# Latent attention in a hybrid decoder layer: values projected in token order, keys in a bank of their own, a new order of splits, and all ten turns of a head's probabilities behind the gate

## What is computed

```python
q = (rms_norm(c_q, q_norm) @ w_uq).reshape(b, s, MLA_HEADS, QK_NOPE + QK_ROPE)      # 8 heads, 64 + 32
q_nope, q_pe = q[..., :QK_NOPE], q[..., QK_NOPE:]
q_pe = apply_rope(q_pe, cos[:, :, None], sin[:, :, None])
kv = (rms_norm(c_kv, kv_norm) @ w_ukv).reshape(b, s, MLA_HEADS, QK_NOPE + V_DIM)    # 64 + 64
k_nope, v = kv[..., :QK_NOPE], kv[..., QK_NOPE:]
...
y_a = causal_dense_attention(q_full, k_full, v, (QK_NOPE + QK_ROPE) ** -0.5) @ w_br_mla
```

## Time and profile before

| | |
|---|---|
| median of 3 runs | 1281.73 us (1281.72 to 1281.84) |
| the profiled execution | 1280.79 us, its span 1279.0 us |
| PE busy | 1267.3 us (99%) |
| DVE, ACT, POOL busy | 669.7, 441.7, 18.8 us |

### The profile page before, as it was taken

One profiled execution on the slowest core, in us unless ns is written; L12 is line 12 of the kernel. 1 busy time (PEld: TensorE's weight loads), 2 busy tenths in 40 slices (PEclk: granted clock), 3 DMA queues, 4 the chain that ended last, 5 costly groups with the idle time before them and its releaser, 6 DMA issues.

```text
span 1279.0 us, 16611 instructions
## 1 busy us (share of the span) xinstructions
PE 1267.3 (99%) x5998; PEld 1033.5 (81%) x5998; DVE 669.7 (52%) x984; ACT 441.7 (35%) x763; POOL 18.8 (1%) x36
## 2 busy tenths in 40 slices
PE   9999999999999999999999999999999999999997
PEld 6888888888888777788888888888888888888886
DVE  6744444433336677475665746675644444443323
ACT  6233332322233444343343424423433332232221
POOL 0000000000000000300000000000000000000000
PEclk9999999999999999999999999999999999999999
DMA  6342223333322221622222231222322322233321
GB/s 214 101 111 98 98 98 98 90 91 95 103 92 71 64 70 66 132 67 83 79 78 92 66 99 51 97 89 95 99 96 98 98 98 98 98 90 92 93 88 66
DMA packets 36003, 118.38 MB, mean 93 GB/s; under 512 B 4680, under 2 KB 4680, under 8 KB 35968
## 3 DMA queue, kind: packets, MB, share of 16 engines
q1 hardware_dynamic: 34416, 114.83, 27.8%
q0 software_dynamic: 1264, 3.06, 1.5%
q10 hardware_dynamic: 288, 0.03, 0.0%
HBM read 115.36 MB, written 2.55 MB: 92 GB/s over the span
## 4 chain that ended last, share of the span: by engine, by line
PE 94%; DVE 2%; DMA 1%; issue 1%; ACT 1%; SPq 0%; DVEq 0%; ACTq 0%
PE bank L542 36%; PE bank L376 17%; PE bank L378 17%; PE bank L377 17%; PE bank L725 1%; PE bank L751 1%; PE bank L645 1%; PE bank L672 1%; DVE mla_stats L1451 1%; DMA x<-in_x_t 1%; PE bank L661 1%; PE bank L769 1%; PE bank L765 1%; DMA const<-in_tables 0%; ACT w_hi L358 0%
## 5 line engine op out<-in xcount | busy, mean ns | idle before, releaser
L363 DVE TENSOR_TENSOR w_lo<-raw,w_hi 128x1024 fp32r<-128x1024 f32 (+2 forms) x221 | 258.8, 1171 | 227.6 <-ACT w_hi L358 225.4
L358 ACT ACTIVATE w_hi<-raw 128x1024 fp32r<-128x1024 f32 (+2 forms) x221 | 224.3, 1015 | 433.3 <-PE bank L542 228.3
L542 PE MATMUL bank<-act_hi,w_hi 128*128 128x512 f32 x704 | 218.5, 392 | 0.3 <-DVE w_lo L363 0.3
L542 PE MATMUL bank<-act_hi,w_lo 128*128 128x512 f32 x704 | 217.0, 389 | 0.0
L542 PE MATMUL bank<-act_lo,w_hi 128*128 128x512 f32 x704 | 216.9, 389 | 0.0
L376 PE MATMUL bank<-act_hi,w_hi 128*128 128x512 f32 x528 | 210.7, 399 | 2.0 <-DVE w_lo L363 1.2
L378 PE MATMUL bank<-act_hi,w_lo 128*128 128x512 f32 x528 | 206.2, 390 | 0.0
L377 PE MATMUL bank<-act_lo,w_hi 128*128 128x512 f32 x528 | 205.9, 390 | 0.0
L542 PEld LDWEIGHTS bank<-act_hi,w_hi 128*128 128x128 f32 x704 | 132.2, 188 | 29.6 <-DVE w_lo L363 1.0
L542 PEld LDWEIGHTS bank<-act_hi,w_lo 128*128 128x128 f32 x704 | 132.2, 188 | 27.5
L542 PEld LDWEIGHTS bank<-act_lo,w_hi 128*128 128x128 f32 x704 | 132.2, 188 | 27.4
(11 more groups left out here) (177 smaller groups left out, 1049.3 us busy)
## 6 DMA issues: line engine op xcount, KB each, us to landing
raw<-in_ffn_up SPq DMA_DIRECT2D x87, 512.0 KB, 3.3
raw<-in_w_dil SPq DMA_DIRECT2D x40, 512.0 KB, 3.3
raw<-in_ffn_down SPq DMA_DIRECT2D x32, 448.0 KB, 3.3
raw<-in_ffn_down SPq DMA_DIRECT2D x16, 512.0 KB, 3.5
raw<-in_w_mla_gates SPq DMA_DIRECT2D x8, 512.0 KB, 3.3
raw<-in_w_branches SPq DMA_DIRECT2D x8, 512.0 KB, 3.3
raw<-in_w_out SPq DMA_DIRECT2D x8, 512.0 KB, 3.2
raw<-in_w_latent SPq DMA_DIRECT2D x6, 512.0 KB, 3.3
```

The source lines that it names most:

```text
L358: nc.scalar.activation(w_hi[:, s % SPLIT, 0:tiles * P], raw[:, s % RAW, 0:tiles * P], ACT.Copy).then_inc(hi_ready, 1)
L363: nc.vector.tensor_tensor(w_lo[:, s % SPLIT, 0:tiles * P], raw[:, s % RAW, 0:tiles * P], w_hi[:, s % SPLIT, 0:tiles * P].bitcast(F32), ALU ...
L542: last = nc.tensor.matmul(out, w[:, s % SPLIT, tile * P:(tile + 1) * P], moving[:, row, :], start=row == 0 and w is w_hi and moving is act_hi,
```

## The change

All values are now projected at once before head 0, with the latents as the stationary operand, so that they come out in token order (`values`, 24 products into banks 5, 6, 2, 3) and are scaled and copied by ACT (`take_values`). The transposes of values and the tensor `mla_vt` are gone. The first of two heads projects keys for both (6 products into bank 7, which `attend` uses as well); queries always go to bank 0 and gates to bank 1. The ten transposes of a head's probabilities all stand behind the gate, in banks 5, 6 and 0. ACT splits the next gate's piece before the tanh; in even heads DVE takes the query before it normalizes; in the last head the split of the second dilated piece moves ahead of exponentials and normalizing. In the first SwiGLU the split of piece 4 moves ahead by half a turn. The loop over heads is written out.

```diff
+            def values():
+                s = PIECES["mla"]
+                pe.wait_ge(lo_ready, s + 1)
+                pe.wait_ge(chunk_taken, CHUNKS["latent"] + 4)
+                for b, out in enumerate((5, 6, 2, 3)):
+                    block_of = slice(b * P, (b + 1) * P)
+                    for k in range(KKV):
+                        hi, lo = (w[:, s % SPLIT, k * SEQ:(k + 1) * SEQ] for w in (w_hi, w_lo))
+                        latent, rest = (part[:, KQ + k, block_of] for part in (lat_hi, lat_lo))
+                        nc.tensor.matmul(bank[out][:, :], latent, hi, start=k == 0, stop=False)
+                        nc.tensor.matmul(bank[out][:, :], latent, lo, start=False, stop=False)
+                        last = nc.tensor.matmul(bank[out][:, :], rest, hi, start=False, stop=k == KKV - 1)
...
+            def lora(h):
+                s = lora_piece(h)
+                pe.wait_ge(lo_ready, s + 1)
+                if h % 2 == 0:
+                    if h == 0:
+                        pe.wait_ge(mean_ready, 2)
+                    elif h > 2:
+                        pe.wait_ge(mixed_taken, h // 2 - 1)
+                    multiply(s, range(KQ, LORA_TILES), bank[7][:, :], ...).then_inc(inner_done, 1)
+                c = query_chunk(h)
+                free_chunk(pe, c)
+                if h > 1:
+                    pe.wait_ge(turned_taken, 3 * (h - 1))
+                multiply(s, range(KQ), bank[c % 2][:, :], ...).then_inc(piece_done, 1)
-            def turn_values(h, i):
...
             def turn_probs(h, part):
+                unit = 3 * h + part
+                pe.wait_ge(mla_scaled, 4 * h + 4)
+                if h:
+                    pe.wait_ge(turned_taken, unit - 2)
+                if part == 2:
+                    pe.wait_ge(chunk_taken, (query_chunk(h + 1) if h < MLA_HEADS - 1 else CHUNKS["dil"]) + 1)
...
             def attend(h):
+                if h < MLA_HEADS - 1:
+                    pe.wait_ge(keys_taken, h // 2 + 2)
                 for key in range(BLOCKS):
...
-                    pe.wait_ge(turned_taken, 4 * h + 2 + part + 8 * i)
+                    pe.wait_ge(turned_taken, 3 * h + 1 + part)
...
             def attention(h):
                 score(h)
-                turn_values(h, i)
-                def turn_early(k):
-                    if k == 6:
-                        turn_probs(h, i, 0)
-                        turn_probs(h, i, 1)
                 if h < MLA_HEADS - 1:
-                    project(s + 1, d, c + 6 * i, bank[c % 2][:, :], turn_early)
+                    lora(h + 1)
+                    project(lora_piece(h + 1) + 1, 0, c, bank[c % 2][:, :])
...
-                turn_probs(h, i, 2)
+                for part in range(3):
+                    turn_probs(h, part)
                 if h % 2:
+                    attend(h)
...
 # ACT
+            def attention(h):
                 if h == MLA_HEADS - 1:
+                    split_hi(act, PIECES["dil"] + 1, 0, TILES)
+                exponentials(h)
+                if h < MLA_HEADS - 2:
+                    split_hi(act, lora_piece(h + 2), 0, lora_tiles(h))
+                elif h == MLA_HEADS - 2:
+                    split_hi(act, PIECES["dil"], 0, TILES)
+                else:
+                    split_hi(act, PIECES["dil"] + 2, 0, TILES)
+                take_probs(h)
+                if h < MLA_HEADS - 2:
+                    split_hi(act, lora_piece(h + 2) + 1, 0, TILES)
...
 # DVE
+            def attention(h):
+                maxima(h)
...
+                    if h % 2:
+                        take_keys(h // 2 + 1)
+                        normalize(h)
+                        take_query(h + 1)
+                    else:
+                        take_query(h + 1)
+                        normalize(h)
```

More of the change, by code:

```diff
@@ L428, in _ @@
                 load(sp, PIECES["latent"] + q, 0, w_latent[q], TILES)
[L430 to L439, removed]
+            load(sp, PIECES["mla"], 0, w_values, TILES)
+            for h in range(MLA_HEADS):
+                at, tiles = (h % 2) * LORA_TILES * P, lora_tiles(h)
+                load(sp, lora_piece(h), 0, w_lora_up[h // 2, :, at:at + tiles * P], tiles)
+                load(sp, lora_piece(h) + 1, 0, w_mla_gates[h], TILES)
             with sp.Fori(0, PAIRS) as i:
@@ L609, in _ @@
             token_sums(sumsq, bank[7]).then_inc(norm_full, 1)
[L612 to L620, removed]
@@ L622, in turn_values @@
-            def turn_values(h, i):
[L625 to L640, removed]
+            def values():
[10 more added lines that the diff above has]
+                        last = nc.tensor.matmul(bank[out][:, :], rest, hi, start=False, stop=k == KKV - 1)
+                    if b < BLOCKS - 1:
+                        last.then_inc(values_done, 1)
+                last.then_inc(piece_done, 1)
@@ L641, in score @@
+            def score(h):
+                pe.wait_ge(head_ready, h + 1)
+                if h == 0:
+                    pe.wait_ge(values_taken, BLOCKS)
                 for b, (out, diagonal) in enumerate(((bank[2][:, 0:P], bank[2][:, 0:P]),
@@ L1255, in up_turn @@
                             dve.wait_ge(own, so_far())
-                    else:
+                    elif not (first and f == 0):
                         split_lo(dve, s + 2, 4 * i, TILES)
@@ L1261, in up_turn @@
                     nc.vector.tensor_tensor(work[:, 0, :], bank[c % UP_BANKS][:, :], rstd[:, :], ALU.mult).then_inc(chunk_taken, 1)
-                    if not (first and f == 0 and j == 0):
+                    if first and f == 0 and j == 0:
+                        split_lo(dve, s + 4, 0, TILES)
+                    else:
                         split_lo(dve, s + 3, 4 * i, DOWN_PARTS[1][1] - DOWN_PARTS[1][0] if last and j else TILES)
@@ new lines, in take_query, with take_keys @@
+                dve.wait_ge(chunk_taken, c + 1)
+                nc.vector.tensor_tensor(out[low, :], out[low, :], rotated[low, :], ALU.add).then_inc(head_ready, 1)
+            def take_keys(p):
+                source = bank[7]
+                dve.wait_ge(inner_done, p + 1)
+                nc.vector.tensor_tensor(mla_k[0:QK_NOPE, 0, :], source[0:QK_NOPE, :], rstd_kv[0:QK_NOPE, :], ALU.mult)
+                nc.vector.tensor_tensor(mla_k[0:QK_NOPE, 1, :], source[QK_NOPE:P, :], rstd_kv[QK_NOPE:P, :], ALU.mult)\
+                  .then_inc(keys_taken, 1)
@@ L1780 @@
     up_q = given["w_uq"][0].reshape(Q_LORA, MLA_HEADS, QK_DIM)
-    up_kv = _tiles(given["w_ukv"][0])
+    up_kv = given["w_ukv"][0].reshape(KV_LORA, MLA_HEADS, QK_NOPE + V_DIM)
+    put("w_values", up_kv[:, :, QK_NOPE:].reshape(KKV, P, MLA_HEADS * V_DIM).transpose(1, 0, 2).reshape(P, TILES * P))
     rows = []
-    for h in range(MLA_HEADS):
-        query = np.concatenate([up_q[:, h, :QK_NOPE], _swapped(up_q[:, h, QK_NOPE:])], axis=1)
-        rows.append(np.concatenate([_tiles(query)[0], up_kv[h]], axis=1))
+    for pair in range(MLA_HEADS // 2):
+        first, second = (_tiles(np.concatenate([up_q[:, h, :QK_NOPE], _swapped(up_q[:, h, QK_NOPE:])], axis=1))[0]
+                         for h in (2 * pair, 2 * pair + 1))
+        keys = _tiles(up_kv[:, 2 * pair:2 * pair + 2, :QK_NOPE].reshape(KV_LORA, 2 * QK_NOPE))[0]
+        rows.append(np.concatenate([first, keys, second], axis=1))
     put("w_lora_up", np.stack(rows))
```

217 lines of the change are left out of this document (98 added, 119 removed).

## The result

The median of the changed kernel is 1273.7 us (4 runs, 1273.23 to 1274.22), that of the kernel before in the same comparison 1281.78 us (4 runs, 1281.72 to 1283.47): a ratio of 0.9934 (0.9917 to 0.9951), 8.1 us less. The prediction was 1276.2 us with a range from 1274.3 to 1279.3. The profiled execution took 1274.22 us, where the sum gave 1275.3.

The account below looks back on a forecast made before the run. PE was taken to bound the kernel, busy 99% of the span. 3.0 + 1.43 + 1.33 + 0.28 + 0.64 - 1.2 = 5.5 us won, giving 1275.3 profiled and 1276.2 us as median, range 1274.3 to 1279.3.

Parts of the forecast that it names:

- turned values, eight heads: Between last mask and first `lora` product: four uncovered small transposes per head go, 0.38 us each head, 3.0 us won.
- gates of heads 0, 1, 3, 5: PE no longer waits at these gates for the bank shared with next keys and values; 1.43 us won.
- last head: PE no longer waits for w_lo of the second dilated piece, split before exponentials and normalizing; all 1.33 us won.
- first turn: First SwiGLU: piece 4's split moves ahead of a silu, so PE's wait for it goes; 0.28 us won.
- turns together, less attend's wait: Ten transposes in one row win 0.64 us over eight heads; attend waiting for ACT's copy loses 1.2 in odd heads.
- What bounds the kernel: Whole kernel: PE, busy 99% of the span; time is won only if PE issues less or waits less.
- The products that move: Keys and values: 24 products go and 24 come at 0.227 us each, 5.45 us both ways; nothing won or lost.
- That rival: Attend in odd heads waits for all three ACT copies: 3.0 us more, 1279.2; chance 0.10 including something between.
- The slower rival: DVE's chain in heads 1, 3 and 5 is late, PE loses 2.9 us three times: 1284.9; chance 0.05.
- Given back: A later wait, such as bias-table transfers or fetching written-out code, takes back what is won: 1281.7; chance 0.07.
- More is won: In the heads, attend's wait is hidden and the turns give 1.1 us: 1274.5; chance 0.12.

## Why the prediction was off: its steps against the traces

| step | forecast | measured | how read |
|---|---|---|---|
| turned values, eight heads | 3.0 | 3.9 | 0.49 a head: 0.10 to them, 0.39 themselves |
| gates of heads 0, 1, 3, 5 | 1.43 | 2.2 | 33 products behind the turned values: 8.36 and 3 x 8.09, in heads without a wait 7.61; 0.7 of it by the loop written out |
| last head | 1.33 | 1.64 | 48 products: 11.15 + 1.48 before, 10.99 now; 0.11 of it is a change between kinds of product |
| first turn | 0.28 | 0.35 | 1.09 to 0.74 |
| turns together, less attend's wait | -0.56 | -0.60 | even heads +0.02, odd -0.17 |
| ahead of head 0 | 0 | 0.28 | 39 products 9.18 to 8.84, less 0.06 for the values; 0.2 of it is the gap of 0.06 and its 0.13 |
| sum | 5.5 | 7.8 | 7.43 + 0.35 |

Between the two profiled spans it is 6.6 and not 7.8, since the start was 1.16 us later in the profile of after (22.18 against 21.02 for the token sums). Behind the stage both are alike: 742.15 and 742.18 us.

- **What bounds the kernel** held: all that was won is PE's, and all of it stayed won.
- **The products that move** cost next to nothing: the values take 0.232 us each with their entry, nearly the value taken (0.227), 0.06 us in all.
- **The steps that failed are "Turned values go" and "The gate no longer waits for a bank".** The direction of both is right and the price too small: I priced each by its gap alone, from one start to the next, 3.0 and 1.43 us, where 3.9 and 2.2 were won. The runs show a cost beside the gap. The step from the mask to the turned values was 0.10 longer than to a full product (shown by taking four such turns out and putting them back), and the products behind a wait take 0.13 to 0.14 more in all (shown by the wait put back). These are 0.9 us and most of 0.8, and 0.2 of the last head's is of the same kind. I compared the step of 0.38 with nothing and took it as the whole. The cause given for the second step is right in part only: of its 1.43 us of gap some 0.8 go when nothing but the loop is written out, with the bank still shared. The prediction counted the loop at nothing; the total held for it only because the change does both.
- **Turns together and attend's wait** came to -0.60 for -0.56, partly by luck. In even heads the turns won 0.02 us and not 0.08: one change between kinds of product goes, 0.11, but ten turns to the next score take 1.09 where seven and three took 1.01. Odd heads lost 0.17 and not 0.22, in head 7 only 0.06 once its 0.11 in the row above is counted here. The 1.37 us to attend held in heads 1, 3 and 5, a sum of 0.64 + 0.587 + 0.14 from three rows. ACT's first copy is what attend waits for, not all three: attend starts at 446.40, when the copies that began at 445.67 still have 0.6 us to go. That rival is out.
- **The slower rival**, DVE's chain late in odd heads, did not come: the gates and turns stand in no list of waits, and in head 1 the third query operation was over at 444.59, before the first turn. **Given back** did not come either; the written-out loop even won 0.2 us in three heads.
- **More is won** came, at 1273.7 and not 1274.5, and by another way than I gave it: I let it rest on the turns and on attend, whose sum held. The lower end of the range put the low bounds of those together (they give 1274.5, not 1274.3) and gave the two well-seen steps no room below. A range must also hold the error of terms that seem read off.

## What to carry to other kernels

The price of a stall or of an odd instruction on a saturated engine is not its gap: take the distance over some twenty instructions around it, with and without it (a neighbour head without the stall does for that), and the 0.1 to 0.2 us beside the gap come along. A part that takes work away ahead of a wait wins nothing until the wait goes too: turned values were worth 1.1 us alone and 3.9 with bank and last head changed. And a change of half a microsecond is judged in its window of the trace, when the start of the run varies by 1.8 and one drop of the clock costs 1.5.

## What the runs showed of the hardware

Going from a product over 128 rows to a transpose of 64 by 64 costs 0.09 us on entry in both places tried, and four such turns cost a head 0.52 us where four of twice the rows and columns cost 0.39 to 0.41. Products of 128x512 behind a gap in TensorE's stream lose 0.13 to 0.18 us in all behind gaps of 0.04 to 1.1 us, and 0.09 behind one of 1.88; most of it lies in the first step, and the gap can be too short for any list. Why is not shown by any run. With the loop on all engines DVE's taking of keys and values ends 0.15 us later behind the score of head 1 (436.87 less 430.11, against 436.92 less 430.31), and PE starts 0.08 later behind it (0.14 against 0.06); which instructions do it stays open. Once the granted clock fell to its lower level behind the token sums, for eight products and 1.50 us. The version with early turns in odd heads is shorter in the stage by 0.5 us, and whether it beats the changed kernel as a whole is not decided (1274.26 and 1273.7 us).
